# Attention: one PSUM bank for the values, four for the scores, and the scores made two steps ahead

## The reference

```python
s = jnp.einsum('bqgrd,bqkgd->bgrqk', qc, kg) * scale
p = masked_softmax(s, mask)
o = jnp.einsum('bgrqk,bqkgd->bqgrd', p, vg)
```

## Time and profile before

| | |
|---|---|
| Three runs | 2590.79, 2594.11, 2598.24 us; median 2594.11 |
| Profiled execution | 2598.19 us, of which the span 2596.5 us |
| Mean granted clock of TensorE in it | 0.972 of 2.4 GHz |
| Attention 0 | from scores(0) at 201.0 to the first panel of the projection at 297.2 us |
| Attention 1 | 861.1 to 969.0 us |
| Attention 2 | 2085.4 to 2169.9 us |

### The profile page before, as it was taken

How to read it: one execution, slowest core, us unless ns; L and a number is a source line. 1 busy time by engine, 2 the same in 40 slices (tenths; PEclk the granted TensorE clock), 3 DMA queues, 4 the chain that set the end, 5 groups by cost and what they waited for, 6 DMA issues and landing times.

```text
span 2596.5 us, 35948 instructions
## 1 busy us (share of the span) xinstructions
PE 2467.6 (95%) x12239; PEld 2029.2 (78%) x12239; DVE 1357.2 (52%) x2511; ACT 918.5 (35%) x1466; POOL 941.2 (36%) x405
## 2 busy tenths in 40 slices
PE   8897979999999899999999969999999999999998
PEld 7776868888877677888888758888878978888886
DVE  6568764444156865111117775635356565545445
ACT  3245423222233353322234434322236364432222
POOL 2220114444443102444444624444444401444443
PEclk9998989999999899999999979999999999999999
DMA  7430135545222102322222203322222201232322
GB/s 304 178 134 33 50 125 199 187 178 178 91 88 84 39 1 106 105 97 96 95 92 99 72 26 112 104 90 97 97 97 97 90 34 41 81 105 89 105 89 73
DMA packets 64335, 263.55 MB, mean 102 GB/s; under 512 B 7264, under 2 KB 7776, under 8 KB 57952
## 3 DMA queue, kind: packets, MB, share of 16 engines
q1 hardware_dynamic: 61056, 251.00, 27.7%
q10 hardware_dynamic: 3168, 11.08, 1.2%
HBM read 259.95 MB, written 2.10 MB: 101 GB/s over the span
## 4 chain that ended last, share of the span: by engine, by line
PE 79%; issue 8%; DVE 7%; ACT 2%; POOL 1%; DMA 1%; DVEq 1%; POOLq 0%; ACTq 0%; SPq 0%
PE bank L594 23%; PE bank L596 23%; PE bank L595 23%; PE bank L768 4%; PE bank L746 2%; PE bank L756 2%; POOL w_lo L565 1%; DMA modraw<-in_pairs 1%; DVE bank L2115 1%; DVE bank L1758 1%; DVE acc L1482 1%; PE bank L697 0%; DVE iacc L2048 0%; DVE cval L1599 0%; PE bank L781 0%
## 5 line engine op out<-in xcount | busy, mean ns | idle before, releaser
L565 POOL TENSOR_TENSOR w_lo<-raw,w_hi 128x1024 fp32r<-128x1024 f32 x378 | 911.1, 2417 | 1627.6 <-ACT w_hi L1118 1626.7
L594 PE MATMUL bank<-h_hi,w_hi 128*128 128x512 f32 x1760 | 701.0, 398 | 27.3 <-DVE h_lo L1529 7.8
L595 PE MATMUL bank<-h_lo,w_hi 128*128 128x512 f32 x1760 | 692.4, 393 | 0.0
L596 PE MATMUL bank<-h_hi,w_lo 128*128 128x512 f32 x1760 | 692.1, 393 | 0.0
L1118 ACT ACTIVATE w_hi<-raw 128x1024 fp32r<-128x1024 f32 x378 | 393.5, 1052 | 521.9 <-PE bank L596 519.1
L594 PE MATMUL bank<-g_hi,w_hi 128*128 128x512 f32 x1072 | 419.7, 391 | 5.6 <-DVE g_lo L1634 5.6
L594 PEld LDWEIGHTS bank<-h_hi,w_hi 128*128 128x128 f32 x1760 | 335.0, 190 | 108.2 <-issue 8.8
L596 PE MATMUL bank<-g_hi,w_lo 128*128 128x512 f32 x1072 | 417.9, 390 | 0.0
L595 PE MATMUL bank<-g_lo,w_hi 128*128 128x512 f32 x1072 | 417.7, 390 | 0.0
L596 PEld LDWEIGHTS bank<-h_hi,w_lo 128*128 128x128 f32 x1760 | 335.0, 190 | 71.7
L595 PEld LDWEIGHTS bank<-h_lo,w_hi 128*128 128x128 f32 x1760 | 335.4, 191 | 69.0 <-issue 0.5
(11 more groups left out here) (294 smaller groups left out, 2647.1 us busy)
## 6 DMA issues: line engine op xcount, KB each, us to landing
raw<-in_panels SPq DMA_DIRECT2D x378, 512.0 KB, 3.2
modraw<-in_pairs SPq DMA_DIRECT2D x40, 1024.0 KB, 5.4
first_mods<-in_first SPq DMA_DIRECT2D x4, 2048.0 KB, 21.2
w<-in_w ACTq DMA_DIRECT2D x2, 2048.0 KB, 8.7
x<-in_x SPq DMA_DIRECT2D x1, 2048.0 KB, 8.1
out<-yout ACTq DMA_DIRECT2D x8, 256.0 KB, 2.1
mask<-in_causal ACTq DMA_DIRECT2D x1, 1024.0 KB, 4.9
mask<-in_dilated ACTq DMA_DIRECT2D x1, 1024.0 KB, 5.0
```

Of the source, the lines that this page charges most:

```text
L565: pool.tensor_tensor(w_lo[:, slot, :], raw[:, slot, :], w_hi[:, slot, :].bitcast(F32), ALU.subtract)\
L594: pe.matmul(out, w_h, m_h, start=start, stop=False)
L595: pe.matmul(out, w_h, m_l, start=False, stop=False)
L596: return pe.matmul(out, w_l, m_h, start=False, stop=stop)
```

## The change

The values of all steps go to bank 4, which frees bank 5 for a fourth scores bank. Scores(n) now reuse the banks of scores(n - 2) and wait for both masks of that step. Scores(0) and scores(1) are made before the loop; in it, scores(n + 2) stand behind turning(n) and ahead of values(n - 1). Values(n) wait for the output of step n - 1. VectorE and ScalarE keep their order; only their bank numbers change.

```diff
--- before.py
+++ after.py
@@ -509,7 +509,9 @@
 
             return [(m, i, r) for m, (i, r) in enumerate(TURN_ORDER) if TURNED_AT[run][m] == n]
 
-        SBANK = (0, 1, 6)
+        SBANK = (0, 1, 5, 6)
+
+        VBANK = 4
 
 
         @block.sync
@@ -739,11 +741,11 @@
 
                 def scores(n):
 
-                    if n:
-                        pe.wait_ge(masked_ready, 2 * (at + n) - 1)
+                    if n >= 2:
+                        pe.wait_ge(masked_ready, 2 * (at + n) - 2)
                     w = P * (pairs_[n][0] + 1)
                     for b in range(2):
-                        pe.matmul(bank[SBANK[(2 * n + b) % 3]][:, 0:w], q_of(run, pairs_[n], b), k_of(run, pairs_[n], b),
+                        pe.matmul(bank[SBANK[(2 * n + b) % 4]][:, 0:w], q_of(run, pairs_[n], b), k_of(run, pairs_[n], b),
                                   start=True, stop=True).then_inc(score_ready, 1)
 
                 def turn(n):
@@ -759,13 +761,13 @@
 
                 def values(n):
 
-                    if n >= 2:
-                        pe.wait_ge(o_done, at + n - 1)
+                    if n:
+                        pe.wait_ge(o_done, at + n)
                     last = pairs_[n][0]
                     for b, copied in enumerate((pt_even, pt_odd)):
                         pe.wait_ge(copied, at + n + 1)
                         for j in range(last + 1):
-                            m = pe.matmul(bank[4 + n % 2][:, HD * b:HD * b + HD],
+                            m = pe.matmul(bank[VBANK][:, HD * b:HD * b + HD],
                                           probT[:, 2 * (n % 2) + b, P * j:P * j + P], v_of(run, pairs_[n], b, j),
                                           start=(j == 0), stop=(j == last))
                     m.then_inc(pv_done, 1)
@@ -794,10 +796,11 @@
                         m.then_inc(panel_done, 1)
 
                 scores(0)
+                scores(1)
                 for n in range(N_PAIR):
-                    if n + 1 < N_PAIR:
-                        scores(n + 1)
                     turn(n)
+                    if n + 2 < N_PAIR:
+                        scores(n + 2)
                     if n:
                         values(n - 1)
                     for m, i, r in rounds_at(run, n):
@@ -1661,7 +1664,7 @@
                     dve.wait_ge(score_ready, u + 1)
                     if n >= 2:
                         dve.wait_ge(pt_done, u - 3)
-                    dve.tensor_tensor_reduce(prob[:, 2 * (n % 2) + b, 0:w], bank[SBANK[(2 * n + b) % 3]][:, 0:w], mask[:, i, 0:w],
+                    dve.tensor_tensor_reduce(prob[:, 2 * (n % 2) + b, 0:w], bank[SBANK[(2 * n + b) % 4]][:, 0:w], mask[:, i, 0:w],
                                              -SCALE, HIGHEST, ADD, ALU.min, stat[:, 0, u % 64:u % 64 + 1])\
                         .then_inc(masked_ready, 1)
 
@@ -1689,7 +1692,7 @@
                         dve.tensor_tensor(factor, factor, gate, MUL)
                         dve.drain()
                     dve.wait_ge(pv_done, at + n + 1)
-                    of = bank[4 + n % 2][:, 0:2 * HD]
+                    of = bank[VBANK][:, 0:2 * HD]
                     if run == 0:
                         for b in range(2):
                             o = o_of(run, pairs_[n], b)
```

## The result

| | before | after |
|---|---|---|
| Median of five runs each, taken side by side | 2598.24 us | 2616.09 us |
| Ratio | | 1.007, 95% interval 1.0054 to 1.0085 |
| Profiled execution, its span | 2598.19, 2596.5 us | 2616.09, 2614.4 us |
| Mean granted clock | 0.972 | 0.966 |
| Attention 0 | 96.1 us | 99.0 us |

The change made the kernel slower by 0.7%; the forecast of 2596.0 us missed it and its range (to 2604) too. The attentions (first scores to first projection panel) hold 15.6 of the 17.9 us between the two spans. Attention 0 starts 2.1 us later in a part of the program that is the same in both; over the traces of this study that start lies anywhere from 199.2 to 203.1 us.

The account below looks back on a forecast made before the run. TensorE, busy 95% of the span, was taken to bound the kernel. Terms 0 + 0 + 0.2 + 1.7 + 0 = +1.9 us on the 2594.11 us median gave 2596.0 us, range 2587 to 2604 us.

Parts of the forecast that it names:

- Attention 1 beside the picks: Attention 1, where VectorE also does the picks: taken as 0, best case -11.8 us, worst +3.3 or, with several stretches, +7.
- Base: Starting time of the forecast: 2594.11 us, the median of the runs shown; the profiled execution took 2598.19 us.
- Border of scores between turning and values: TensorE's switches between 64-row and 128-row groups, all attentions: taken as 0, bounds -0.10 to +0.10 us a step.
- the prediction's own sign of being wrong: Repeated TensorE wait before values, pair-of-steps period other than 5.00 us, or the 866 to 922 us stretch shorter by 5+.
- Tail: End of each attention: values(31) wait for output(30), +0.69 us in attention 0, +0.50 in 1 and 2, sum 1.7 us.
- Values bank in the steps: One values bank adds a wait for output(n-1); only four-block values in attention 0 fall short, 0.03 us 8 times: 0.2 us.
- Scores two ahead: Scores two steps ahead in four banks: no TensorE wait to remove in attentions 0 and 2 but at the start; 0 us.
- The first rival: Attention 1 gains as VectorE's 8.5 us of waits go: 2584.2 us if all, 2590.1 if half; chance 0.14.
- The second: Values bank stalls TensorE at four-block values of each first half: 0.4 us in 24 steps, +9.6, 2605.6 us; chance 0.10.
- The third, the clock: TensorE's rests shift before turning(0) and in attention 1, adding half-rate time: +1.7 to +5 us, 2598 to 2601; chance 0.08.

Follow-up runs that it names:

- the fourth trace: The changed kernel run once more with nothing edited, the last of three later executions of it: 2604.45 us.

## Why the prediction was wrong

Two steps of the prediction failed, both terms put at nothing. The border between scores and turning was taken as 0 and cost 4.9 us. Attention 1 beside the picks was taken as 0, with +7 as its worst case, and cost 10.5 us in the profiled execution, most of it by more time at half rate. Base, border and tail alone make 2596.0 + 4.1 + 4.9 + 0.6 = 2605.6 us, just outside the range; attention 1 brought the rest.

**Base.** The three runs shown had their median at 2594.11 us; later sets of before had 2597.9 to 2599.5. So 4 of the 20 us between forecast and result are the base; against the profiled execution the forecast said 2600.1.

**Border of scores between turning and values.** I took 0 between bounds of -0.10 and +0.10 us a step. It measured +0.05: 1.6 us an attention, 4.9 us in all. The argument was that turning and values are alike, both with full-array weights at 0.11 us a row, so that scores could follow either at the same price. They couldn't here: behind a turning they cost 0.04 to 0.05 us more than behind values. The price was half of the upper bound, so the bound held, and the prediction's own sign of being wrong (a period other than 5.00) came true. The constant of 0.21 us that I split between borders isn't two borders of 0.10 either; parting the scores showed 0.06 to 0.07. Beside the picks this price needn't show: two of the four traces have 90.1 and 90.2 us in the last column of the table, against 89.9 before, and in the profiled execution TensorE rested 2.4 us less in exchange.

**Tail.** 1.7 us forecast; 1.13 + 0.59 + 0.59 = 2.3 measured. The waits for the last output came as worked out. Missed was that in attention 0 values(30) wait too, 0.34 us for output(29), once the last scores are gone.

**Values bank in the steps.** 0.2 us forecast. In the change no such wait shows in attention 0 or 2, so the arithmetic of need and cover held there (the cover of values A is 0.74 us now, 2122.62 to 2123.36, as much as the need). In the old order it was about 1 us, where a values row was 0.1 longer.

**Scores two ahead: 0.** Right in its size and reason. TensorE waited for nothing in attention 0 and 2, and scores truly one step earlier gained nothing anywhere. What the edit calls two steps ahead is, but for the start, an exchange of scores with values(n-1); with the two put back (scores behind values) the order is that of before.

**Attention 1 beside the picks: taken as 0, worst case +7.** It measured +10.5 in the profiled execution, and 9.5 between the medians of the change and of the run with the old order there (2616.1 and 2606.6). The three later executions of the change (2604.5 to 2611.8) bring the median of all eight to 2611.6, 5.0 above that run, so 10 is the upper part of what it costs, and the fourth trace (attention 1 108.3 us) shows that it can be next to nothing. I had seen that values get late, and had weighed only VectorE's waits (4.8 us, now 10.8). These cost nothing by themselves: without picks they are there (12.2 us) and attention 1 differs by 2.2 us, its border and tail. The price beside the picks came through the clock, which I had put at one to three stretches of about 3 us without asking what a little more lateness does to a part that already stood at 0.82. The first rival (attention 1 gains) is refuted: the waits for masks went, as it said, but came back in front of the turnings. The second (the bank stalls TensorE) holds only for scores ahead of turning. The third, the clock, had the right mechanism with +5 as its end, where up to +10 was to be had. The range was also not half way to the rivals, as it said of itself: 2587 is 9 of the 11.8 us to the first, 2604 is 8 of the 9.6 us to the second.

The sum as it should have been: 4.9 + 2.3 = 7.2 us for border and tail, which the two kernels without picks show (7.7). Beside the picks up to 2.2 of them are covered, and 0 to 10 us come by the clock.

**What stays open.** Why the clock falls at one rest of TensorE in attention 1 and not at the next, and so how the order brings the long loss in some executions. Between the first and the 17th turning of attention 1 TensorE's rests are fewer and shorter in sum than before (5.3 against 7.7 us, counting those over 0.15 us), though the longest is longer (1.86 against 1.52). Their sum isn't what decides. Also why the first two pairs of attention 0 take 4.5 us more in some traces.

## What to carry to other kernels

Where TensorE never waits, more lookahead is worth nothing, and each exchange of groups has a price at its borders: look at what follows what, start to start, and don't put a border that no row shows at zero. Here 0.05 us a step made 4.9 us. Where an in-order engine is near its limit, put work that is ready ahead of work that waits for another engine; here that one exchange on VectorE (picks ahead of the output) brought 0.2%, while the lookahead lost 0.7%. And where a stretch already stands partly at half rate, let the range hold a good deal more of it; here 25 us became up to 45, worth 10 us.

## What the runs showed of the hardware

- Two matmuls of 64 rows on the two halves of the array ran side by side: 1.06 us for the pair, 1.05 us for one alone, 512 columns each. With other work between them they took twice that.
- TensorE's clock can stay at half without a rest: with the scores parted it was busy 93.5 of 93.5 us at 0.50 in attention 2 (pairs of 12.61 us), while the same pairs ran at 1.00 in attention 0 (6.84 us).
- In attention 1 of the change TensorE's clock fell to half three times behind its first turning, though no rest was longer than 1.86 us from there on.
- Executions of one program differ by up to 20 us here (2599.85 to 2620.23), and the time follows the mean granted clock (0.972 to 0.964). The traces show single stretches of half rate that are there in one execution and not in the next. A single trace of such a kernel isn't enough to say what a change did to a stretch.
